# Prompt attention in one inference step: a third score buffer, another order of ScalarE's copies, one head's weighting on GpSimd

## The chip, the cores and the metric

The kernel runs on one core of a Trainium2 chip. The metric is the device time in microseconds, the median of several runs. The engines are TensorE (PE), VectorE (DVE), ScalarE (ACT), GpSimd (POOL) and SyncE (SP), which here only issues DMAs.

## What is computed

One layer of a decoder for 1024 prompt tokens and 8 x 4 sample tokens: a gated MLP mixer beside a sparse attention with three branches, an output projection, a cross attention, a gated MLP with a convolution. The change lies in the prompt's sparse attention. It has 8 query heads of width 64 and 2 key heads. Cut to what matters:

```python
l_cmp = einsum(q, kc) * scale + bias(d_cmp)        # 63 compressed keys
p_cmp = masked_softmax(l_cmp, d_cmp >= 0)
l_sel = einsum(q, k_sel) * scale + bias(d_sel)     # selected blocks, causal
p_sel = masked_softmax(l_sel, m_sel)
p_win = masked_softmax(einsum(q, k_band) * scale + bias(dist), 0 <= dist < 512)
out   = g0 * p_cmp @ vc + g1 * p_sel @ v_sel + g2 * p_win @ v_band
```

With 1024 tokens every causal block of 64 is among the selected ones, so the second branch is full causal attention.

## The kernel before

`program` runs phases one after the other, each a block of per-engine programs whose order is written out by hand and tied by semaphores: input, gating, compression, `sample_attention` (L633), `prompt_attention` (L835), then the output mix and the rest. A barrier ends each block.

**The steps.** `prompt_attention` works through 32 steps (`STEPS`, L852). Step m has a head pair j (0 to 3: query heads j and j + 4, called head g = 0 and g = 1) and a query block i of 128 tokens. For even j, i goes 0 to 7, for odd j 7 to 0. One head of a step has a score row of up to 1727 columns in SBUF: (i+1) x 128 "far" scores (second branch), min(i+1, 5) x 128 window scores and 63 compressed ones, the last two together called "near". In blocks of up to 128 columns that is 3, 5, 7, 9, 11, 12, 13 and 14 blocks for i = 0 to 7. `groups` (L861) cuts them into groups of four: one to three groups for i up to 5, four for i = 6 and 7.

**What each engine does in pass m** (loops over m at L946, L992 and L1039):

- PE: transposes of head 1 of step m-2 (`turn`, L928), near scores of m (L913, L917), the product with the values of m-2 (`multiply`, L941), far scores of m+1 (L901), transposes of head 0 of step m-1.
- DVE: `far` adds the bias to the far scores of m for both heads and takes the minimum (`add`, L961), from PSUM to the score buffer `sc`; `weigh` for head 0 of m-1: a reciprocal (L985) and three TENSOR_SCALAR (L988) that multiply the exponents by 1/sum and the gate; `close` adds the bias to the near scores of both heads (two adds each, L961); `weigh` for head 1 of m-1.
- ACT: copies of the transposed head 1 of m-2 from PSUM to SBUF (`copy`, L1027, L1030), exponents of head 0 of m (three ACTIVATE, L1018), the finished output of m-2 (L1037), copies of head 0 of m-1, exponents of head 1 of m. As written, the copy of head 1 of a step thus stands behind the exponents of head 1 of the next step.

**Buffers.** Scores land in PSUM banks 0 to 3, far and near in the same ones: near scores wait for `far_taken` (both far adds done), far scores of the next step for `near_taken` (all close adds done). Transposes go to banks 4 to 6, one group each: the group with number t waits until the group t-3 is copied (L926). Outputs are in bank 7. `sc` has two buffers for each head (L844), so `far` of step n waits until the transposes of the same head of step n-2 are done (L967).

**Strips.** The bias comes as strips, 960 KB and 320 KB for each head (`near`, `inside`), one set for each head pair, from `bias_rows` in DRAM (L879, L880). SP issues the sets of j = 0 and 1 at the start of the block, then the reload of x (L885, three DMAs, needed by the output mix), then the sets of j = 2 and 3 when their places are free. In the block before, SP issues page loads (`gather`) only; PE there computes products for two halves of the samples (L726) and counts them in `pv`.

The lines that say most:

```python
pe.wait_ge(copied, t - 2)                                                       # L926, t >= 3
dve.wait_ge(turned, turns[n - 2, g, len(groups(n - 2)) - 1] + 1)                # L967, n >= 2
```

Of the kernel before, what the change touches and what calls it, by code (L numbers as in the profile page):

```python
# [632 lines left out]
def sample_attention(nc, K, I):  # L633
# [27 lines left out]
    with nc.Block() as block:  # L661
        @block.sync
        def _(sp):
            gather(sp, K, 1, "sel")

# [168 lines left out]

def prompt_attention(nc, K, I):  # L835
# [4 lines left out]
    near = [[ar[:, 2560 * g:2560 * g + STRS] for g in range(2)],  # L840
            [ar[:, 5120 + STRS * g:5120 + STRS * (g + 1)] for g in range(2)]]
    inside = [[ar[:, 2560 * g + STRS:2560 * (g + 1)] for g in range(2)],
              [K.top[:, O_CP + 192 + STRW * g:O_CP + 192 + STRW * (g + 1)] for g in range(2)]]
    sc = [[ar[:, 8960 + 1728 * (2 * b + g):8960 + 1728 * (2 * b + g + 1)] for g in range(2)] for b in range(2)]  # L844
    pt = [x.rearrange("p (b n) -> p b n", b=14) for x in (K.top[:, O_TMP:O_TMP + 1792], ar[:, 15872:17664])]
    sta = [[ar[:, 17664 + 16 * (2 * b + g):17664 + 16 * (2 * b + g + 1)] for g in range(2)] for b in range(2)]
    strip_came = [S(f"pa_strip{b}") for b in range(2)]
    far_done, far_taken, near_done, near_taken = S("pa_far"), S("pa_far_taken"), S("pa_near"), S("pa_near_taken")
    minima, exps, probs = S("pa_minima"), S("pa_exp"), S("pa_probs")
# [23 lines left out]
    with nc.Block() as block:  # L873
        @block.sync
        def _(sp):
            def strip(j):
                for g in range(2):
                    base = (j + 4 * g) * (VECS + VECW)
                    sp.dma_start(near[j % 2][g], bass.AP(K.vec_dram.tensor, base, [[1, P], [1, STRS]])).then_inc(strip_came[j % 2], 16)  # L879
                    sp.dma_start(inside[j % 2][g], bass.AP(K.vec_dram.tensor, base + VECS, [[1, P], [1, STRW]])).then_inc(strip_came[j % 2], 16)  # L880

            strip(0)
            strip(1)
            for a, b in PIECES:
                sp.dma_start(K.XT[:, :, a:b], I["xt"][:, :, a:b]).then_inc(K.x_came, 16)  # L885
            for j in range(2, 4):
                sp.wait_ge(near_taken, 8 * (j - 1))
                strip(j)

        @block.tensor  # L890
        def _(pe):
# [29 lines left out]
            def turn(n, g):  # L921
                pe.wait_ge(probs, 2 * n + g + 1)
                for k, (_, bl) in enumerate(groups(n)):
                    t = turns[n, g, k]
                    if t >= 3:
                        pe.wait_ge(copied, t - 2)  # L926
                    for x, (col, w, _, _) in enumerate(bl):
                        last = nc.tensor.transpose(K.bank[4 + t % 3][:w, x * P:(x + 1) * P], sc[n % 2][g][:, col:col + w], K.ident[:, :])  # L928
# [30 lines left out]
        def _(dve):  # L959
# [4 lines left out]
            def far(n, g):  # L964
                j, i = STEPS[n]
                if n >= 2:
                    dve.wait_ge(turned, turns[n - 2, g, len(groups(n - 2)) - 1] + 1)  # L967
                w = (i + 1) * P
                return add(sc[n % 2][g][:, 0:w], K.ps[:, 1024 * g:1024 * g + w], near[j % 2][g][:, 895 + w:895:-1], sta[n % 2][g][:, 1:2])

            def close(n, g):
                j, i = STEPS[n]
                s, m, strip = sc[n % 2][g], sta[n % 2][g], near[j % 2][g]
                w = min(i + 1, 5) * P
                top = 992 + P * i
                add(s[:, 1024:1024 + w], K.ps[:, 1024 * g:1024 * g + w], inside[j % 2][g][:, w - 1::-1], m[:, 2:3])
# [3 lines left out]
            def weigh(n, g):  # L980
                j, i = STEPS[n]
                s, m = sc[n % 2][g], sta[n % 2][g]
# [7 lines left out]
                last.then_inc(probs, 1)  # L990

            for n in range(N):  # L992
                j, i = STEPS[n]
                if n % 8 == 0:
                    dve.wait_ge(strip_came[j % 2], 64 * (j // 2 + 1))
# [14 lines left out]

        @block.scalar
        def _(act):
            def exp(n, g):
                _, i = STEPS[n]
                s, m = sc[n % 2][g], sta[n % 2][g]
# [23 lines left out]
            for m in range(N + 2):  # L1039
                if m >= 2:  # L1040
                    copy(m - 2, 1)
# [4 lines left out]
                if 1 <= m <= N:  # L1046
                    copy(m - 1, 0)
                if m < N:
# [846 lines left out]
def program(nc, I, O):  # L1895
    ctx = ExitStack()
    with ctx:
# [56 lines left out]
        K.sample_o = K.big[:, BIG - 256:BIG].rearrange("p (h n) -> p h n", h=2)  # L1954
        K.pools = {"cmp": I["pool_cmp"], "sel": I["pool_sel"]}
# [207 lines left out]
```

## Time and profile before

| | us |
|---|---|
| median of 3 runs (lowest, highest) | 2157.05 (2155.07, 2157.63) |
| the profiled execution's own time | 2156.39 |
| its span, first to last instruction | 2154.6 |
| PE busy in the span | 1960.8 (91%) |
| DVE / ACT / POOL busy | 851.6 / 507.4 / 221.4 |
| mean granted TensorE clock (1 is 2.4 GHz) | 0.958 |

Times in rows count from the span's start. The prompt attention runs from about 473 to 791 us, some 15% of the span. An interval between the near scores of two steps is the unit in which it moves. Matmul ends are modelled, so the start of the next instruction tells more than a duration.

### The profile page before, as it was taken

What the parts mean: (1) busy time and instruction counts of PE and PEld (TensorE: products, weight loads), DVE (VectorE), ACT (ScalarE), POOL (GpSimd) and SP (SyncE); (2) the same over time, 40 slices, a digit from 0 to 9 for tenths busy, and PEclk for the clock granted to TensorE, in tenths of its full rate; (3) what the DMA queues carried; (4) which work ended last, traced back from release to release, by engine and by line L of the source; (5) the groups of instructions that cost most, each with busy time, mean ns of one, the idle gap of its engine ahead of it and who ended that gap; (6) DMA issues with size and microseconds to landing.
All of it is one profiled execution on the core that took longest, in us unless ns stands there. A gap on an engine that the chain in (4) does not pass through costs nothing. (4 is left out here: it accounts for less than half of the span.)

```text
span 2154.6 us, 26289 instructions
## 1 busy us (share of the span) xinstructions
PE 1960.8 (91%) x10926; PEld 1548.8 (72%) x10926; DVE 851.6 (40%) x1832; ACT 507.4 (24%) x1103; POOL 221.4 (10%) x98
## 2 busy tenths in 40 slices
PE   7989998748788869989988899999999999999997
PEld 4555547535565546565658446899999999999997
DVE  3001214236567553530004113455545555545547
ACT  2112221006577561100112102121101111111112
POOL 0000000000000000000000000043223332233230
PEclk9999999867899889999999999999999999999999
DMA  5511006723110020031121600111011110111012
GB/s 208 148 63 71 0 0 168 216 96 112 50 50 1 1 99 39 1 126 60 30 97 40 265 28 0 37 66 54 25 40 59 59 50 11 59 59 59 20 44 81
DMA packets 97003, 145.12 MB, mean 67 GB/s; under 512 B 40622, under 2 KB 73454, under 8 KB 94990
## 3 DMA queue, kind: packets, MB, share of 16 engines
q1 hardware_dynamic: 92798, 140.30, 19.2%
q10 hardware_dynamic: 4088, 3.17, 0.5%
q8 instruction: 86, 1.41, 0.3%
q14 instruction: 31, 0.25, 0.0%
HBM read 132.37 MB, written 14.19 MB: 68 GB/s over the span
## 5 line engine op out<-in xcount | busy, mean ns | idle before, releaser
L1619 PE MATMUL ps<-ff_in_high,ff_weights_low 128*128 128x352 f32 x1056 | 342.6, 324 | 0.0
L1619 PE MATMUL ps<-ff_in_high,ff_weights_high 128*128 128x352 f32 x1056 | 340.2, 322 | 0.0
L1619 PE MATMUL ps<-ff_in_low,ff_weights_high 128*128 128x352 f32 x1056 | 338.0, 320 | 0.0
L1619 PEld LDWEIGHTS ps<-ff_in_high,ff_weights_high 128*128 128x128 f32 x1056 | 198.8, 188 | 0.3
L1619 PEld LDWEIGHTS ps<-ff_in_low,ff_weights_high 128*128 128x128 f32 x1056 | 198.3, 188 | 0.2
L1619 PEld LDWEIGHTS ps<-ff_in_high,ff_weights_low 128*128 128x128 f32 x1056 | 198.1, 188 | 0.0
L1823 DVE TENSOR_TENSOR x<-ps,x 128x352 f32<-128x352 f32 x216 | 113.4, 525 | 134.5 <-PE ps L1637 134.5
L373 PE MATMUL ps<-big 128*128 128x512 f32 (+3 forms) x432 | 160.8, 534 | 6.2 <-DVE top L406 6.2
L1637 PE MATMUL ps<-ff_act_high,ff_down_high 128*128 128x352 f32 (+1 forms) x496 | 158.3, 319 | 0.2
L1637 PE MATMUL ps<-ff_act_high,ff_down_low 128*128 128x352 f32 (+1 forms) x496 | 156.6, 316 | 0.0
L1637 PE MATMUL ps<-ff_act_low,ff_down_high 128*128 128x352 f32 (+1 forms) x496 | 156.5, 316 | 0.0
L1588 POOL TENSOR_TENSOR ff_weights_low<-ff_weights,ff_weights_high 128x1024 fp32r<-128x1024 f32 x44 | 106.0, 2410 | 471.9 <-ACT ff_weights_high L1719 471.9
L373 PEld LDWEIGHTS ps<-big 128*128 128x128 f32 (+1 forms) x432 | 78.8, 183 | 87.1 <-issue 79.9
L1018 ACT ACTIVATE big<-big 128x63 f32<-128x63 f32 (+8 forms) x192 | 114.4, 601 | 77.7 <-DVE big L961 77.4
L1227 PE MATMUL ps<-big 128*128 128x352 f32 x384 | 122.0, 478 | 7.5 <-DVE big L1161 5.5
L961 DVE CUSTOM_DVE_ANT_0 big<-ps,big 128x63 f32<-128x63 f32 (+8 forms) x160 | 81.7, 536 | 109.6 <-PE ps L928 92.5
L1688 PE MATMUL ps<-big 128*128 128x352 f32 x384 | 115.6, 463 | 1.3 <-PEq L1429 1.3
L265 PE MATMUL ps<-big,top 128*128 128x352 f32 x384 | 115.1, 460 | 0.9 <-DMA top<-in_w_fm 0.9
L1273 PE MATMUL ps<-big,top 128*128 128x352 f32 x384 | 113.8, 459 | 0.0
L1227 PEld LDWEIGHTS ps<-big 128*128 128x128 f32 x384 | 75.4, 198 | 50.6 <-issue 8.1
L265 PEld LDWEIGHTS ps<-big,top 128*128 128x128 f32 x384 | 72.5, 190 | 44.8 <-ACT top L238 3.4
L1688 PEld LDWEIGHTS ps<-big 128*128 128x128 f32 x384 | 73.7, 192 | 42.6 <-issue 2.7
(273 smaller groups left out, 2901.7 us busy)
## 6 DMA issues: line engine op xcount, KB each, us to landing
ff_weights<-in_w_up SPq DMA_DIRECT2D x22, 512.0 KB, 4.1
ff_weights<-in_w_gate SPq DMA_DIRECT2D x22, 512.0 KB, 4.3
ff_down<-in_w_down SPq DMA_DIRECT2D x22, 512.0 KB, 3.5
x<-in_xt SPq DMA_DIRECT2D x6, 1408.0 KB, 14.3
big<-bias_rows SPq DMA_DIRECT2D x8, 960.0 KB, 7.7
top<-in_mem_kt SPq DMA_DIRECT2D x7, 1024.0 KB, 11.0
big<-in_w_tm SPq DMA_DIRECT2D x8, 652.0 KB, 16.5
top<-in_mem_v SPq DMA_DIRECT2D x5, 1024.0 KB, 17.3
```

What stands on the lines that cost most here:

```text
L265: last = nc.tensor.matmul(K.bank[3 * (c % 2) + p][:, 0:b - a], ring[:, c % 2, k, :], K.HT[:, k, a:b], start=k == 0, stop=k == KD - 1)
L373: last = nc.tensor.matmul(K.bank[3 * (t % 2) + s][:r, 0:b - a], K.HT[:, k, t * P:t * P + r], w[:, k, a:b], start=k == 0, stop=k == KD - 1)
L961: return nc.vector.tensor_tensor_reduce(out=out, in0=scores, in1=bias, scale=1.0, scalar=3e38, op0=ALU.add, op1=ALU.min, accum_out=least)
L1018: nc.scalar.activation(s[:, x:y], s[:, x:y], ACT.Exp, bias=m[:, b:b + 1], scale=-1.0, accum_out=m[:, 8 + b:9 + b]).then_inc(exps, 1)
L1227: last = nc.tensor.matmul(K.bank[n % 4][:, 0:b - a], w[:, c, k, :], K.HT[:, k, a:b], start=k == 0, stop=k == KD - 1)
L1273: last = nc.tensor.matmul(K.bank[QB[c % 2][p]][:, 0:b - a], xq_ring[:, c % 2, k, :], K.HT[:, k, a:b], start=k == 0, stop=k == KD - 1)
L1588: nc.gpsimd.tensor_tensor(w_low[:, s], landing[:, s], w_high[:, s], ALU.subtract).then_inc(low_done[s], 1)
L1619: last = nc.tensor.matmul(K.bank[3 * s + x][:, 0:b - a], wt[:, s, ws], h[:, k, a:b], start=k + n == 0, stop=k == KD - 1 and n == 2)
L1637: last = nc.tensor.matmul(bank[:, 0:b - a], wt[:, at], x[:, c % SLOTS, a:b], start=first and e + m == 0, stop=end and c == chunks[-1] and ...
L1688: last = nc.tensor.matmul(K.bank[(6, 7, 1, 4)[n % 4]][:, 0:b - a], w[:, c, k, :], K.HT[:, k, a:b], start=k == 0, stop=k == KD - 1)
L1823: nc.vector.tensor_tensor(K.XT[:, o, a:b], K.bank[6 + n % 2][:, 0:b - a], K.XT[:, o, a:b], ALU.add).then_inc(down_taken, 1)
```

## The change

It touches four things. The score buffers `sc` and the statistics become three per head (`SC = 3`), and `far` waits for step n-3. ACT copies head 1 of m-1 right behind head 0 of m-1, ahead of the exponents of head 1 of m. The three TENSOR_SCALAR of head 1 move to a new GpSimd program; DVE keeps the reciprocal, and `probs` becomes one semaphore for each head. And the places are laid out anew: strips of even j go to x's place (`K.first_strips`), so the first set is issued in the sample attention's SP program once the first product there is done, and the reload of x comes last, after 24 steps. Also, `multiply` of n waits for the output copy of n-1 where it waited for n-4.

```diff
@@ sample_attention
         def _(sp):
             gather(sp, K, 1, "sel")
+            sp.wait_ge(pv, 1)
+            bias_strips(sp, K, 0, *K.first_strips)
...
+def bias_strips(sp, K, j, near, inside, came):
+
+    for g in range(2):
+        base = (j + 4 * g) * (VECS + VECW)
+        sp.dma_start(near[g], bass.AP(K.vec_dram.tensor, base, [[1, P], [1, STRS]])).then_inc(came, 16)
+        sp.dma_start(inside[g], bass.AP(K.vec_dram.tensor, base + VECS, [[1, P], [1, STRW]])).then_inc(came, 16)
...
+    first = K.first_strips
+    strips = (first, second, first, second)
+    SC = 3
...
-            strip(0)
-            strip(1)
+            bias_strips(sp, K, 1, *strips[1])
+            for j in range(2, 4):
+                sp.wait_ge(near_taken, 8 * (j - 1))
+                bias_strips(sp, K, j, *strips[j])
+            sp.wait_ge(near_taken, 24)
             for a, b in PIECES:
                 sp.dma_start(K.XT[:, :, a:b], I["xt"][:, :, a:b]).then_inc(K.x_came, 16)
-            for j in range(2, 4):
-                sp.wait_ge(near_taken, 8 * (j - 1))
-                strip(j)
...
             def turn(n, g):
-                pe.wait_ge(probs, 2 * n + g + 1)
+                pe.wait_ge(probs[g], n + 1)
...
             def multiply(n):
-                if n >= 4:
-                    pe.wait_ge(o_taken, n - 3)
+                if n:
+                    pe.wait_ge(o_taken, n)
...
             def far(n, g):
                 j, i = STEPS[n]
-                if n >= 2:
-                    dve.wait_ge(turned, turns[n - 2, g, len(groups(n - 2)) - 1] + 1)
+                if n >= SC:
+                    dve.wait_ge(turned, turns[n - SC, g, len(groups(n - SC)) - 1] + 1)
...
             def weigh(n, g):
...
                 nc.vector.reciprocal(m[:, 12:15], m[:, 8:11]).then_inc(factors, 1)
+                if g:
+                    return
                 dve.wait_ge(factors, 2 * n + g + 1)
...
-                last.then_inc(probs, 1)
+                last.then_inc(probs[0], 1)
...
+        @block.gpsimd
+        def _(pool):
+            for n, (j, i) in enumerate(STEPS):
+                s, m = sc[n % SC][1], sta[n % SC][1]
+                pool.wait_ge(factors, 2 * n + 2)
+                for b, x, y in ((1, 0, (i + 1) * P), (2, 1024, 1024 + min(i + 1, 5) * P), (0, 1664, 1664 + NCMP)):
+                    last = nc.gpsimd.tensor_scalar(s[:, x:y], s[:, x:y], m[:, 12 + b:13 + b], K.GS[:, j + 4, i, b:b + 1],
+                                                   ALU.mult, ALU.mult)
+                last.then_inc(probs[1], 1)
...
             for m in range(N + 2):
-                if m >= 2:
-                    copy(m - 2, 1)
                 if m < N:
                     exp(m, 0)
                 if m >= 2:
                     out(m - 2)
                 if 1 <= m <= N:
                     copy(m - 1, 0)
+                    copy(m - 1, 1)
                 if m < N:
                     exp(m, 1)
```

How the order moves, at the two places on which most rests. First ACT, pass m = 24: L1018 is an exponent, L1037 the output of step 22, L1027 and L1030 copies of step 23, to `top` for head 0 and to `big` for head 1. Before:

```order
L1018 ACTIVATE big<-big 128x1024 [waits pa_minima]
L1018 ACTIVATE big<-big 128x640
L1018 ACTIVATE big<-big 128x63
L1037 ACTIVATE top<-ps 128x128 [waits pa_pv]
L1027 COPY top<-ps 128x512 [waits pa_turned] x3
L1027 COPY top<-ps 128x128 [waits pa_turned]
L1030 COPY top<-ps 63x128
L1018 ACTIVATE big<-big 128x1024 [waits pa_minima]
L1018 ACTIVATE big<-big 128x640
L1018 ACTIVATE big<-big 128x63
L1027 COPY big<-ps 128x512 [waits pa_turned] x3
```

The same place in the changed kernel (its lines are 16 further on):

```order
L1034 ACTIVATE big<-big 128x1024 [waits pa_minima]
L1034 ACTIVATE big<-big 128x640
L1034 ACTIVATE big<-big 128x63
L1053 ACTIVATE top<-ps 128x128 [waits pa_pv]
L1043 COPY top<-ps 128x512 [waits pa_turned] x3
L1043 COPY top<-ps 128x128 [waits pa_turned]
L1046 COPY top<-ps 63x128
L1043 COPY big<-ps 128x512 [waits pa_turned] x3
L1043 COPY big<-ps 128x128 [waits pa_turned]
L1046 COPY big<-ps 63x128
L1034 ACTIVATE big<-big 128x1024 [waits pa_minima]
```

The copies of head 1 moved ahead of the exponents of the next step's head 1.

Second DVE, from the last close add of step 22 to the far adds of step 23 (ISA is the custom add; the row without an input reads its minimum). Before:

```order
L961 ISA big<-ps,big 128x63
L961 ISA big 128x1
L985 RECIPROCAL big<-big 128x3 [waits pa_minima,pa_exp]
L988 TENSOR_SCALAR big<-big,gates_by_head 128x768 [waits pa_factors]
L988 TENSOR_SCALAR big<-big,gates_by_head 128x640
L988 TENSOR_SCALAR big<-big,gates_by_head 128x63
L961 ISA big<-ps,big 128x1024 [waits pa_turned,pa_far]
```

The changed kernel:

```order
L965 ISA big<-ps,x 128x63
L965 ISA big 128x1
L989 RECIPROCAL big<-big 128x3 [waits pa_minima,pa_exp]
L965 ISA big<-ps,x 128x1024 [waits pa_turned,pa_far]
```

Head 1's three multiplications left DVE's queue, and the wait on `pa_turned` now means step 20 where it meant step 21.

## Rows read from the trace of the kernel before

**Rows 1.** Windows view of three stretches: length, busy us (count) of five engines, PEclk, DMA.

```profile
484.00:791.00 307.00, 253.32 (x2284) 184.53 (x2284) 186.34 (x636) 201.82 (x632) 0.00 (x0) 0.90 0.11 39
637.00:688.00 51.00, 42.15 (x384) 28.81 (x384) 39.04 (x139) 38.33 (x130) 0.00 (x0) 1.00 0.09 33
716.00:722.00 6.00, 5.50 (x38) 4.36 (x40) 4.54 (x16) 1.68 (x4) 0.00 (x0) 0.50 0.00 0
```

**Rows 2.** Waits view, 484 to 791 us: us in total, times, longest.

```profile
DVE big L961 <- PE ps L928: 92.5, 52, 4.4
...
PE ps L913 <- DVE big L961: 37.5, 32, 9.6
...
PE ps L928 <- ACT big L1027: 14.3, 8, 1.9
```

**Rows 3.** Timeline of PE, 678 to 702 us: start us, us, engine, line, operation, idle before.

```profile
678.06 1.35 PE L913 MATMUL ps<-top 64*128 64x512 f32 x8 [1.19 <-DVE big L961]
...
684.13 3.00 PE L928 MATMUL ps<-ident,big 128*128 128x128 f32 x24
688.46 1.35 PE L913 MATMUL ps<-top 64*128 64x512 f32 x8 [1.33 <-DVE big L961]
...
689.91 0.32 PE L941 MATMUL ps<-top 128*64 128x128 f32 x1
...
692.83 1.99 PE L901 MATMUL ps<-top 64*128 64x512 f32 x8
694.74 1.65 PE L928 MATMUL ps<-ident,big 128*128 128x128 f32 x13
...
699.95 0.32 PE L928 MATMUL ps<-ident,big 128*63 128x128 f32 x1 [1.79 <-ACT big L1027]
701.59 1.02 PE L913 MATMUL ps<-top 64*128 64x512 f32 x2 [1.33 <-DVE big L961]
```

**Rows 4.** Timeline of DVE and ACT, 689 to 702 us.

```profile
691.70 0.26 DVE L961 CUSTOM_DVE_ANT_0 big<-ps,big 128x63 f32<-128x63 f32 x1
...
697.03 1.16 ACT L1018 ACTIVATE big<-big 128x1024 f32<-128x1024 f32 x1
...
699.32 1.54 ACT L1027 COPY big<-ps 128x512 f32<-128x512 f32 x3
...
700.30 1.23 DVE L961 CUSTOM_DVE_ANT_0 big<-ps,big 128x1024 f32<-128x1024 f32 x1 [2.49 <-PE ps L928]
```

**Rows 5.** Timeline of PE: near scores that start intervals 7, 11, 27 and 31.

```profile
540.54 0.70 PE L913 MATMUL ps<-top 64*128 64x512 f32 x2 [1.33 <-DVE big L961]
...
598.42 1.13 PE L913 MATMUL ps<-top 64*128 64x512 f32 x4 [0.92 <-DVE big L961]
...
746.28 1.22 PE L913 MATMUL ps<-top 64*128 64x512 f32 x2 [0.92 <-DVE big L961]
...
779.19 0.49 PE L913 MATMUL ps<-top 64*128 64x128 f32 x4 [0.39 <-DVE big L961]
```

**Rows 6.** Timeline around the stage's start: PE, SP and DVE.

```profile
448.51 2.00 PE L726 MATMUL ps<-top,big 32*32 32x128 f32 x56
...
473.63 0.36 SPq L879 DMA_DIRECT2D big<-bias_rows  x1
...
483.25 0.29 DVE L961 CUSTOM_DVE_ANT_0 big<-ps,big 128x128 f32<-128x128 f32 x1 [9.89 <-DMA big<-bias_rows]
...
483.82 0.79 PE L913 MATMUL ps<-top 64*128 64x128 f32 x3 [9.65 <-DVE big L961]
```

**Rows 7.** Timeline of PE, 643 to 645 us: far scores with 384 columns.

```profile
643.89 0.92 PE L901 MATMUL ps<-top 64*128 64x384 f32 x4
```

**Rows 8.** Groups by form: instructions of DVE and GpSimd; busy us, mean ns of one.

```profile
L988 DVE TENSOR_SCALAR big<-big,gates_by_head 128x1024 f32<-128x1024 f32 x8 | 6.5, 813 | 0.3
...
L1588 POOL TENSOR_TENSOR ff_weights_low<-ff_weights,ff_weights_high 128x1024 fp32r<-128x1024 f32 x44 | 106.0, 2410 | 471.9 <-ACT ff_weights_high L1719 471.9
...
L1328 POOL MEMSET top<- 128x2048 f32 x1 | 1.8, 1805 | 710.8 <-POOLq L1083 710.8
```

More of the change, by code:

```diff
@@ L839, in prompt_attention @@
     ar = K.big[:, O_HT:BIG]
[L840 to L847, printed above, removed]
+    first = K.first_strips
+    second = ([ar[:, STRS * g:STRS * (g + 1)] for g in range(2)],
+              [ar[:, 2 * STRS + STRW * g:2 * STRS + STRW * (g + 1)] for g in range(2)], S("pa_strip1"))
+    strips = (first, second, first, second)
+    SC = 3
+    sc = [[ar[:, 5120 + 1728 * (2 * b + g):5120 + 1728 * (2 * b + g + 1)] for g in range(2)] for b in range(SC)]
+    pt = [x.rearrange("p (b n) -> p b n", b=14) for x in (K.top[:, O_TMP:O_TMP + 1792], ar[:, 15488:17280])]
+    sta = [[ar[:, 17280 + 16 * (2 * b + g):17280 + 16 * (2 * b + g + 1)] for g in range(2)] for b in range(SC)]
     far_done, far_taken, near_done, near_taken = S("pa_far"), S("pa_far_taken"), S("pa_near"), S("pa_near_taken")
-    minima, exps, probs = S("pa_minima"), S("pa_exp"), S("pa_probs")
+    minima, exps, probs = S("pa_minima"), S("pa_exp"), [S(f"pa_probs{g}") for g in range(2)]
     factors = S("pa_factors")
@@ L927, in turn @@
                     for x, (col, w, _, _) in enumerate(bl):
-                        last = nc.tensor.transpose(K.bank[4 + t % 3][:w, x * P:(x + 1) * P], sc[n % 2][g][:, col:col + w], K.ident[:, :])
+                        last = nc.tensor.transpose(K.bank[4 + t % 3][:w, x * P:(x + 1) * P], sc[n % SC][g][:, col:col + w], K.ident[:, :])
                     last.then_inc(turned, 1)
             def multiply(n):
-                if n >= 4:
-                    pe.wait_ge(o_taken, n - 3)
+                if n:
+                    pe.wait_ge(o_taken, n)
                 gs = groups(n)
@@ L965, in far @@
                 j, i = STEPS[n]
-                if n >= 2:
-                    dve.wait_ge(turned, turns[n - 2, g, len(groups(n - 2)) - 1] + 1)
+                if n >= SC:
+                    dve.wait_ge(turned, turns[n - SC, g, len(groups(n - SC)) - 1] + 1)
                 w = (i + 1) * P
-                return add(sc[n % 2][g][:, 0:w], K.ps[:, 1024 * g:1024 * g + w], near[j % 2][g][:, 895 + w:895:-1], sta[n % 2][g][:, 1:2])
+                return add(sc[n % SC][g][:, 0:w], K.ps[:, 1024 * g:1024 * g + w], strips[j][0][g][:, 895 + w:895:-1], sta[n % SC][g][:, 1:2])
             def close(n, g):
                 j, i = STEPS[n]
-                s, m, strip = sc[n % 2][g], sta[n % 2][g], near[j % 2][g]
+                s, m, strip = sc[n % SC][g], sta[n % SC][g], strips[j][0][g]
                 w = min(i + 1, 5) * P
                 top = 992 + P * i
-                add(s[:, 1024:1024 + w], K.ps[:, 1024 * g:1024 * g + w], inside[j % 2][g][:, w - 1::-1], m[:, 2:3])
+                add(s[:, 1024:1024 + w], K.ps[:, 1024 * g:1024 * g + w], strips[j][1][g][:, w - 1::-1], m[:, 2:3])
                 return add(s[:, 1664:1664 + NCMP], K.ps[:, 1024 * g + 640:1024 * g + 640 + NCMP],
@@ L994, in _ @@
                 if n % 8 == 0:
-                    dve.wait_ge(strip_came[j % 2], 64 * (j // 2 + 1))
+                    dve.wait_ge(strips[j][2], 64 * (j // 2 + 1))
                 dve.wait_ge(far_done, n + 1)
@@ L1014, in exp @@
                 _, i = STEPS[n]
-                s, m = sc[n % 2][g], sta[n % 2][g]
+                s, m = sc[n % SC][g], sta[n % SC][g]
                 act.wait_ge(minima, 2 * n + g + 1)
```

9 lines of the change are left out of this document (3 added, 6 removed).

## The prediction

> **What bounds the kernel now.** The windows view comes first: what does the prompt attention have to give [rows 1]? From 484 to 791 us PE is busy 253 of 307 us, ACT 202, DVE 186, POOL 0, at a mean granted clock of 0.90. No engine is full, so waits decide. The waits view of the same stretch says which [rows 2]: DVE's add (L961) waits 92.5 us for transposes (L928), the near scores on PE (L913) wait 37.5 us for DVE's add, and transposes wait 14.3 us, in eight places, for ACT's copies (L1027).
>
> One wide interval shows how they hang together. Steps are counted m = 0 to 31, with i the query block (8 steps per head pair, i rising, then falling), and an interval runs from near scores of m to those of m+1. From 688.46 to 701.59 (m = 23, i = 7) PE does near scores of 23, the product of 21, far scores of 24 and both transposes of 22 [rows 3]. All but the last transpose is done by 698.16 (699.95 - 1.79). The last one belongs to a fourth group of head 1. It needs a bank that ACT frees with the first copy of that head (L1027 at 699.32), and this copy stands behind the three exponents that began at 697.03 [rows 4]. PE idles 1.79 us. Only then may DVE overwrite the score buffer: its add starts at 700.30, takes 1.23, and the near scores wait for it, 1.33 us more [rows 3, 4]. Only i = 6 and 7 have four groups (13 and 14 blocks), so this happens after steps 6 to 9 and 22 to 25: intervals 7 to 10 and 23 to 26. They last 57.88 us (540.54 to 598.42) and 57.82 us (688.46 to 746.28) [rows 3, 5], **115.7 us together, a mean of 14.5**. In several of them the granted clock falls as well: it is 0.50 in 716 to 722, right after such a stop [rows 1].
>
> The stage's start is a DMA wait: SP issues the first strip at 473.63 and DVE's first add starts at 483.25, after 9.89 us idle [rows 6].
>
> **The sum.** All steps together: from the near scores of step 0 (483.82) to those of step 31 (779.19) the change has 31 intervals of 295.4 us to work on [rows 5, 6].
>
> *1. What PE itself needs at full clock.* From rows 3: near scores 688.46 to 689.91 = 1.45; product of 12 blocks 689.91 to 692.83 = 2.92, 0.243 a block; far scores with 1024 columns 692.83 to 694.74 = 1.91; 24 transposes 3.00, or 2.93 without the last one's tail, 0.122 each. Far scores with 384 columns take 0.92 against 1.99 for 1024 [rows 3, 7], so 0.21 per 128 columns; near scores shrink at the same rate below 640 columns, to 1.23, 1.03, 0.82, 0.60 for i = 3 to 0. Blocks per step are 3, 5, 7, 9, 11, 12, 13, 14 for i = 0 to 7, 74 a head pair. Over 31 intervals: near 37.3, products 281 x 0.243 = 68.3, far 37.1, transposes 576 x 0.122 = 70.3: 213.0 us.
>
> *2. What stays in the way.* Far and near scores share PSUM banks 0 to 3, so far scores still wait until both heads' close adds are done, and near scores until both far adds are. Wide: the close adds end 3.50 us after the near scores start (691.96) [rows 4], 2.05 after they end; the product (2.92) covers them. Narrow: it doesn't. Working this out for each i (near + 0.15 + close adds + 0.12 against near + product) costs 8.9 us over all steps. Where the DVE chain near, close, far, both far adds is longer than PE's work (i rising, 0 to 3) or the GpSimd chain of point 4 is, it adds another 4.1. Each interval also has a hand-off that no row names: interval 22 (678.06 to 688.46) is 10.40, PE's work in it 1.45 + 11 x 0.243 + 1.91 + 24 x 0.122 = 8.96, the last add 1.23, so 0.2 to 0.3; 0.25 x 31 = 7.8. And the clock is still low in the first three intervals (they make part of the 0.10 that the stage's mean lacks), which I leave in: +6. Sum: 213.0 + 8.9 + 4.1 + 7.8 + 6 = **239.8 us against 295.4, 55.6 less**.
>
> In the eight wide intervals that is 76.5 + 2.0 = 78.5 instead of 115.7, 37.2 less; m = 23 by itself: 1.45 + 2.92 + 1.91 + 26 x 0.122 = 9.45 instead of 13.13. The other 18 us come from the rest, 0.3 to 3 us each, mostly because DVE's far adds now run beside the transposes.
>
> *3. Why the wait is gone: order on ACT and a third buffer.* ACT copies head 1 before the exponents of the next step's head 1, so the fourth group finds a bank. Behind these copies now stand exponents (2.3 us at i = 7, 697.03 to 699.32) [rows 4], needed by the reciprocal behind the next close adds, 3.6 us after the near scores start, against copies that end 0.5 after it and 2.3: 2.8. They fit with 0.8 to spare. ACT's own work in such an interval is 2 x 2.3 + 2 x 1.87 + 0.25 = 8.6 of 9.6, close under PE. A far add waits for the transposes of three steps ago, done long before. o_taken is now awaited one step back; that output copy stands ahead of ACT's copies in the pass before, so it costs nothing.
>
> *4. Head 1's weights on GpSimd.* DVE loses 96 TENSOR_SCALAR (813 ns for 1024 elements [rows 8]), all hidden. In its place stands a chain: near scores, both close adds, reciprocal, three GpSimd instructions, head 1's transposes. At m = 23 GpSimd may start 4.0 us after the near scores and PE wants head 1's probabilities at 1.45 + 2.92 + 1.91 + 1.59 = 7.9: 3.9 us of room for 896 + 640 + 63 elements. No row shows a GpSimd TENSOR_SCALAR. Bounds [rows 8]: MEMSET of 2048 takes 1805 ns, 0.88 an element, without an input; TENSOR_TENSOR of 1024 takes 2410 ns, 2.35 an element, with two inputs. One input lies between: I take 1.5 ns and 0.15 us fixed, 2.9 us here, which is hidden. At 0.88 the sum is 1 us less. At 2.35 (4.2 us) the chain is the longest almost everywhere and the sum **18.4 us more**.
> The Trainium skill (GPSIMD Engine Reference, Engine selection) calls GpSimd about twice as slow for two inputs but "1-input is roughly line-rate". No run here shows that; by it the sum would be the one with the lower bound.
>
> *5. Strips and x.* The first four strip DMAs move to SP behind the first half's product in the sample attention, which ends near 450.5 (448.51 + 2.00) [rows 6]; nothing else is queued there. A strip set lands within 9.6 us, so by about 461, and the first far adds need it at 474.2. **9.1 us less**. The second set is issued at 473.6 as ever, for step 8. The x reload (three DMAs) moves behind the strips of steps 16 to 31 and waits for 24 steps: eight are left before its first reader, over 60 us by the sums above, and a set of strips takes under 10. Nothing.
>
> *6. The end.* The last two passes (11.9 us) have the same chain with GpSimd's three small instructions in it: +0.5.
>
> Sum: -55.6 - 9.1 + 0.5 = -64.2. The profiled execution took 2156.39, which gives 2092.2; the median of the runs, 2157.05, is 0.7 above: **2093 us**.
>
> **Rivals.**
> *A. GpSimd at the two-input price.* +18.4: **2111**. For it: the instruction has two more operands, the per-partition factors. Against: only one long input.
> *B. The clock still falls.* Eight intervals keep near scores and product at 1.2 GHz, as in 716 to 722 [rows 1]: six us at half clock lose 3 us of work, some stretches are shorter, so 2.5 each, +20: **2113**. For: PE still has short stops. Against: the clock is at 0.50 behind stops of 1.8 and 1.3 us close together, which go, and at 1.00 through all of 637 to 688 [rows 1], where only stops such as the 1.19 at 678.06 stand [rows 3].
> *C. DVE and GpSimd shut each other out.* DVE's TENSOR_SCALAR of 1024 takes 813 ns, an add of 1024 takes 1.23 us [rows 4, 8]: DVE runs head 0's weights in a faster way. If one such set per step waited for the rest of GpSimd's, 0.5 us, +15: **2108**. By my times they miss each other: GpSimd ends near 6.9 us into interval 23, and DVE reaches its weights only behind the far adds, at 8.9.
> The Trainium skill (SBUF — State Buffer, Who interferes with whom) says DVE's tensor_scalar can take a port pair that GpSimd needs, as "an exclusive lock". No stretch of this stage has both engines, so the trace neither agrees nor disagrees.
> *D. Slower.* GpSimd's TENSOR_SCALAR is slow enough to be the stage's bound. One head has 35.8 thousand elements per partition over all steps, so each ns an element beyond 2.35 adds up to 35.8 us. The total gain is used up at about 2.35 + (64.2 - 18.4) / 35.8 = 3.6 ns, a 1024 piece of 3.7 us. At twice the two-input price, 4.7 ns, it is 2111 + 84 = **2195**. Against: 2410 ns is the dearer kind of work.
>
> **Chances.** Forecast (with GpSimd cheap or middling) 0.58, A 0.18, B 0.11, C 0.08, D 0.04, no change 0.01. The low end, 2080, is the sum with full clock from the start (-6), the cheap GpSimd (-1) and hand-offs of 0.1 us (-4.7). The high end, 2119, takes in A, B and C and some of their overlap. About 0.2% (4 us) is what a measurement can tell from no change: faster 0.95, same 0.01, slower 0.04.
>
> **What would show it.** Intervals 7 to 10 and 23 to 26 between 9 and 10.5 us, with no PE wait for L1043 longer than 0.5 us and the clock at 1.00 through them; the first far add within 1 us of the first far scores; GpSimd's three instructions within 3.2 us at i = 7 and done before PE ends head 0's transposes. Right in total but wrong in kind: PE waiting for GpSimd (A, D), DVE's TENSOR_SCALAR of 1024 longer than 0.82 us (C), windows at 0.50 beyond the start (B). A time over 2125 makes the working wrong.

## The result, and the profile after

| | before | after |
|---|---|---|
| median us of 4 runs each (lowest, highest) | 2157.10 (2155.07, 2157.63) | **2081.82** (2080.13, 2083.28) |
| ratio to before, 95% interval | | 0.9652 [0.9636, 0.9669] |
| the profiled execution's time, its span | 2156.39, 2154.6 | 2083.28, 2081.5 |
| near scores of step 0, of step 31 | 483.82, 779.19 | 473.58, 704.76 |
| end of the stage's last output copy | 791.05 | 715.61 |

The change saves 75.3 us, 11 more than the 64.2 forecast. The 31 intervals take 231.18 us instead of 295.37, so 64.2 of it is there (by chance the figure of the whole forecast); the stage starts 10.2 us earlier, and its tail, from step 31's near scores to the end of the last output copy, takes 1.0 us less (10.85 for 11.86). The page of the changed kernel shows PE busy 93% of a shorter span, and work on GpSimd from the tenth of the 40 slices on:

```profile
PE 1939.8 (93%) x10926; PEld 1534.3 (74%) x10926; DVE 810.6 (39%) x1736; ACT 505.3 (24%) x1103; POOL 283.6 (14%) x194
...
POOL 0000000002222200000000000313331333133320
PEclk9999999969999999999999999999999999999999
```

The windows view of the changed kernel, which answers to [rows 1] (length, busy us of PE, PEld, DVE, ACT and POOL, PEclk, DMA):

```profile
477.00:480.00 3.00, 1.54 (x8) 1.19 (x8) 2.26 (x13) 0.51 (x3) 0.00 (x0) 0.50 0.95 360
480.00:483.00 3.00, 2.79 (x10) 1.64 (x10) 1.37 (x8) 1.31 (x8) 1.27 (x3) 0.50 0.32 124
483.00:486.00 3.00, 3.00 (x22) 1.86 (x20) 1.72 (x9) 2.10 (x10) 0.00 (x0) 0.60 0.00 0
...
486.00:716.00 230.00, 219.94 (x2238) 163.09 (x2236) 138.67 (x505) 193.61 (x604) 60.95 (x93) 1.00 0.13 43
```

PE is now busy 96% of the stretch (219.94 of 230) where it was 83%, and the granted clock is 1.00 (2.4 GHz) from 486 us to the stage's end. Only the first three intervals are partly at 0.50 (1.2 GHz). The waits view of 473 to 716 us, against [rows 2]:

```profile
DVE big L965 <- PE ps L905: 54.5, 32, 2.7
...
DVE big L965 <- PE ps L921: 28.9, 32, 1.8
...
PE ps L905 <- DVEq L1011: 5.2, 9, 1.3
...
PE ps L932 <- POOL big L1023: 2.5, 5, 0.9
PE ps L932 <- ACT top L1043: 1.9, 8, 0.3
PE ps L917 <- DVE big L965: 1.6, 2, 0.9
```

Three things have gone: DVE waiting for transposes (92.5 us), transposes waiting for head 1's copies (14.3, no row any more), and the near scores waiting for DVE's add (37.5, now 1.6). DVE still waits, but for the scores that it works on, as it should when PE is the bound. What is left for PE is 5.2 us for the close adds ahead of far scores (L1011 is DVE's count behind them), 2.5 us for GpSimd, and little else. Interval 23, of which [rows 3, 4] showed the old form, is now this on PE (timeline: start, us, engine, line, operation, idle before):

```profile
637.19 1.35 PE L917 MATMUL ps<-top 64*128 64x512 f32 x8
...
638.64 0.32 PE L945 MATMUL ps<-top 128*64 128x128 f32 x1
...
641.56 1.99 PE L905 MATMUL ps<-top 64*128 64x512 f32 x8
643.47 1.66 PE L932 MATMUL ps<-ident,big 128*128 128x128 f32 x13
645.38 1.63 PE L932 MATMUL ps<-ident,big 128*128 128x128 f32 x13 [0.25 <-ACT top L1043]
646.94 1.24 PE L917 MATMUL ps<-top 64*128 64x512 f32 x6
```

and this on DVE, ACT and POOL:

```profile
643.69 1.23 DVE L965 CUSTOM_DVE_ANT_0 big<-ps,big 128x1024 f32<-128x1024 f32 x1 [2.67 <-PE ps L905]
...
646.05 1.56 ACT L1043 COPY big<-ps 128x512 f32<-128x512 f32 x3 [0.18 <-PE ps L932]
647.49 0.27 ACT L1046 COPY big<-ps 63x128 f32<-63x128 f32 x1
647.65 1.16 ACT L1034 ACTIVATE big<-big 128x1024 f32<-128x1024 f32 x1
...
641.12 2.34 POOL L1023 TENSOR_SCALAR big<-big,gates_by_head 128x896 f32<-128x896 f32 x3 [6.76 <-DVE big L989]
```

The far add starts at 643.69, beside the transposes, where it used to come after all of them. ACT copies head 1 first and begins the exponents behind (647.65). PE stops once, 0.25 us for a bank, and the interval takes 9.75 us instead of 13.13. GpSimd is done at 643.46, 1.7 us before head 0's transposes end (645.13).

### The profile page after: what moved, and what is told of

The parts are those of the page before. It is cut to its first block and busy times, and to the rows that moved or that the text cites. A ratio compares the mean times of both kernels' runs of the same rounds, so it can differ in the third digit from the quotient of the medians.

```text
span 2081.5 us, 26292 instructions
## 1 busy us (share of the span) xinstructions
PE 1939.8 (93%) x10926; PEld 1534.3 (74%) x10926; DVE 810.6 (39%) x1736; ACT 505.3 (24%) x1103; POOL 283.6 (14%) x194
## 5 line engine op out<-in xcount | busy, mean ns | idle before, releaser
L265 PEld LDWEIGHTS ps<-big,top 128*128 128x128 f32 x384 | 72.5, 190 | 44.9 <-ACT top L238 5.3
L1288 PEld LDWEIGHTS ps<-big,top 128*128 128x128 f32 x384 | 73.0, 190 | 40.9 <-issue 0.5
```

Of the source, the lines that this page charges most:

```text
L265: last = nc.tensor.matmul(K.bank[3 * (c % 2) + p][:, 0:b - a], ring[:, c % 2, k, :], K.HT[:, k, a:b], start=k == 0, stop=k == KD - 1)
L1288: last = nc.tensor.matmul(K.bank[QB[c % 2][p]][:, 0:b - a], xq_ring[:, c % 2, k, :], K.HT[:, k, a:b], start=k == 0, stop=k == KD - 1)
```

## The experiments

Each was timed beside the kernel before on the same chip, in three groups: runs of before had medians of 2154.9 (first group), 2154.2 (second) and 2155.1 (third). Diffs are against the changed kernel unless they say otherwise. Step numbers, intervals and line numbers are those of the changed kernel; where an edit shifts lines, the text says what a line is.

### Group 1: one part undone at a time

**Head 1's weights back on DVE.** Three buffers, the new ACT order and the early strips stay.

```diff
@@ weigh
-                if g:
-                    return
-                last.then_inc(probs[0], 1)
+                last.then_inc(probs[g], 1)
@@ the GpSimd program: removed
```

> The changed kernel with head 1's three multiplications back on DVE, behind its reciprocal. My theory (the third buffer, ACT's order and the early strips carry the gain; GpSimd carries none of it): 2083 to 2088 us, because in the wide intervals DVE has the weights done before the next far scores end, and only in narrow ones (i up to 3) the far adds start some 0.3 us later. Rival (taking work off DVE is part of the gain): 2095 or more. Other rival (GpSimd is a burden and DVE's weights come sooner): under 2080, and the 0.9 us stops of PE before the last transposes of steps 30 and 31 go.

Measured: **2077.33** (2076.84 to 2078.07), ratio 0.9642 [0.9629, 0.9655]. The theory's 2083 to 2088 is a miss, and the second rival is what happened. The median is *lower* than the changed kernel's, though the ratio intervals overlap ([0.9636, 0.9669] there). All intervals are as before the edit but those of the narrowest steps, 15 to 17: 4.42, 3.57, 4.23 instead of 4.67, 3.96, 4.28. The timelines say why. In the changed kernel in interval 15 (PE, then POOL):

```profile
590.83 0.77 PE L932 MATMUL ps<-ident,big 128*128 128x128 f32 x5
591.96 0.77 PE L932 MATMUL ps<-ident,big 128*128 128x128 f32 x5 [0.37 <-POOL big L1023]
...
590.42 1.49 POOL L1023 TENSOR_SCALAR big<-big,gates_by_head 128x256 f32<-128x256 f32 x3 [3.40 <-DVE big L989]
```

and with the weights on DVE:

```profile
591.53 1.65 PE L932 MATMUL ps<-ident,big 128*128 128x128 f32 x10
...
591.06 0.96 DVE L992 TENSOR_SCALAR big<-big,gates_by_head 128x256 f32<-128x256 f32 x3
```

The same three pieces take 0.96 us on DVE and 1.49 on GpSimd, and PE's transposes run through. Intervals 15 to 17 give 0.7 us and the tail, where the changed kernel stops PE for 0.88 and 0.82 us (0.20 and 0.31 here), another 1.2. These 1.9 us stand in the traces; the medians, taken on different chips, are 4.5 apart. DVE had room for its 96 instructions; relieving it was worth nothing.

**Two score buffers.**

```diff
-    SC = 3
+    SC = 2
```

> The changed kernel with two score buffers for each head instead of three. My theory: the near scores again wait for head 1's transposes plus one far add (0.2 to 1.2 us, 0.7 in the mean, and a hand-off of 0.25) in each of 31 intervals: about +25, 2107 us (2100 to 2114), intervals 23 to 26 near 11 us. Rival (ACT's order alone removes the wait, the buffer is an extra): 2082 to 2088.

Measured: **2112.07** (2111.02 to 2112.97), 0.9802 [0.9787, 0.9817], 30 above the changed kernel and inside what was expected. The wide intervals are 11.15, 11.14, 11.0 and 10.55, and the clock stays at 1.00 there. Its waits view has one PE wait that the changed kernel lacks, once in every step, and DVE waits for transposes again:

```profile
DVE big L965 <- PE ps L932: 106.3, 52, 4.4
...
PE ps L917 <- DVE big L965: 28.2, 32, 1.3
```

28.2 us of stops for 31 us more in the intervals (262.3 against 231.2). So the third buffer removes one wait per step, of about the last far add that stood between the last transpose and the near scores (1.3 us where that add takes 1.23).

**The old order of ACT's copies**, with three buffers.

```diff
             for m in range(N + 2):
+                if m >= 2:
+                    copy(m - 2, 1)
                 if m < N:
                     exp(m, 0)
...
                     copy(m - 1, 0)
-                    copy(m - 1, 1)
```

> The changed kernel with ACT's copies of head 1 again behind the exponents of the next step's head 1. My theory: PE stops about 1.8 us in the eight intervals that have a fourth group, +15, 2097 us (2092 to 2106, the high end if the clock falls again), other intervals as they are. Rival (with three buffers the order no longer matters): 2082 to 2085.

Measured: **2113.52** (2109.78 to 2119.44), 0.9819 [0.9802, 0.9836], well above all that was expected. The bank wait is there as expected, 14.3 us in eight places, but there is another one beside it, on the product (L945):

```profile
PE ps L945 <- ACT big L1043: 15.0, 20, 1.5
PE ps L932 <- ACT big L1043: 14.3, 8, 1.9
```

Interval 23 of this kernel shows both on PE's timeline:

```profile
656.59 1.35 PE L917 MATMUL ps<-top 64*128 64x512 f32 x8
...
658.73 0.29 PE L945 MATMUL ps<-top 128*64 128x128 f32 x1 [0.62 <-ACT big L1043]
...
668.76 0.32 PE L932 MATMUL ps<-ident,big 128*63 128x128 f32 x1 [1.79 <-ACT big L1043]
669.02 0.70 PE L917 MATMUL ps<-top 64*128 64x512 f32 x2
```

The product of a step needs all its transposes copied. With the old order head 1's copies stand behind exponents, and PE, which no longer stops for DVE, now reaches the product before they are done. With two buffers nearly all of this wait was covered by the near scores' own. The waits view of the kernel before has only this of it, two of the four places in the tail:

```profile
PE ps L941 <- ACT big L1027: 3.4, 4, 1.5
```

A third buffer with the old order turns 3.4 us in 4 places into 15.0 in 20. The expectation left that out. It did name the clock, and in this profile, the shortest of the four executions, the clock falls too: over 546 to 572 us, where intervals 9 and 10 lie, it averages 0.87, and they take 13.53 and 12.95 us, against 11.92 and 11.32 for intervals 25 and 26, alike but at 1.00. That is 3.2 of the 31 us, and rival B of the prediction in small. The other executions, up to 9.7 us longer, have no profile.

**Strips at the block's start** as before, all else changed.

```diff
-            sp.wait_ge(pv, 1)
-            bias_strips(sp, K, 0, *K.first_strips)
@@ prompt_attention
         def _(sp):
+            bias_strips(sp, K, 0, *strips[0])
```

> The changed kernel with the first set of strips issued at the start of the prompt attention as before. Theory: the first far add starts 10 us later, everything behind it by as much: 2092 us (2090 to 2093). Rival (the rest catches up, or the clock at the start pays it back): under 2088.

Measured: **2090.68** (2089.35 to 2091.65), 0.9702 [0.9687, 0.9717], as expected, 9 us above the changed kernel. That is a net figure: in the profiles the near scores of step 0 come 10.1 us later and the 31 intervals take 233.0 us instead of 231.2, but the part behind the stage, where nothing was edited, happens to be 3.6 us shorter. DVE's first add waits for the DMA again:

```profile
483.13 0.29 DVE L964 CUSTOM_DVE_ANT_0 big<-ps,x 128x128 f32<-128x128 f32 x1 [9.75 <-DMA x<-bias_rows]
```

In the changed kernel it starts at 473.01, 0.65 us after the first far scores (472.36).

### Group 2: parts alone, and a way to mend the cost

**The changed kernel once more**, so that the group has it on its own chip. 

> The changed kernel as it is, on the chip of the next three. 2081 us, or 2079 if the 2.5 us by which its first profile was longer behind the prompt attention belonged to that chip; ratio to the kernel before 0.965.

Measured: 2081.18 (2081.04 to 2084.76), 0.9668 [0.9655, 0.9681].

**Weights on DVE, and PE waiting on the minima** themselves in place of the count that DVE sets after them.

```diff
-                    pe.wait_ge(near_taken, n)
+                    pe.wait_ge(minima, 2 * n)
...
                 close(n, 1).then_inc(minima, 1)
-                dve.wait_ge(minima, 2 * n + 2)
-                dve.sem_inc(near_taken, 1)
@@ weigh for both heads, no GpSimd program; SP waits on minima too
```

> The changed kernel with head 1's weights back on DVE, and with far scores and strips waiting for DVE's close adds themselves (minima) instead of the extra DVE wait and signal (near_taken). Theory: 1 to 3 us under the changed kernel on the same chip: 2.0 from the weights (the two 0.9 us stops at the end and 0.7 in intervals 15 to 17), up to 1 from the hand-off in the dozen narrow intervals that the DVE chain sets. Rival (the 2 us were another chip's): within 1 us of the changed kernel.

Measured: **2077.61** (2076.24 to 2082.47), 0.9652 [0.9638, 0.9666], 3.6 us under the changed kernel on this chip, where 1 to 3 were expected, with ratio intervals that overlap a little. The narrow intervals lose 0.05 to 0.07 each; 229.89 us for the 31, 1.2 less than the changed kernel there (231.05). Nothing else is gained by the shorter hand-off.

**The new ACT order alone, in the kernel before.**

```diff
@@ before
             for m in range(N + 2):
-                if m >= 2:
-                    copy(m - 2, 1)
...
                     copy(m - 1, 0)
+                    copy(m - 1, 1)
```

> The kernel before with nothing changed but ACT's order: copies of both heads ahead of the exponents of the next step's head 1. If the parts add up: the old order cost 31 us in the changed kernel, so 2124 us. My theory: the 1.8 us stops and the late product go, the last far add stays on the path: 2122 (2118 to 2130), intervals 23 to 26 near 11.1 as with two buffers in the changed kernel, since GpSimd plays no part.

Measured: **2118.78** (2117.95 to 2119.62), 0.9838 [0.9823, 0.9853]: 35.4 us under before for three moved lines, as expected. The 31 intervals take 262.5.

**The third buffer alone, in the kernel before**, with the places that it needs, strips at the block's start and both heads' weights on DVE. (It also keeps the semaphores per head and the earlier wait of `multiply`.)

```diff
@@ before
+    SC = 3
...
-                if n >= 2:
-                    dve.wait_ge(turned, turns[n - 2, g, len(groups(n - 2)) - 1] + 1)
+                if n >= SC:
+                    dve.wait_ge(turned, turns[n - SC, g, len(groups(n - SC)) - 1] + 1)
```

> The kernel before with the third score buffer alone (strips of even head pairs in x's place, but the first set issued at the stage's start, x reloaded late; old order on ACT, weights on DVE). If the parts add up: 30 us under the kernel before, 2125. Theory: the same stops as with the old order in the changed kernel, so 2113.5 + 9 for the strips - 2 for the weights = 2120 (2116 to 2126). A rival (buffer and order need each other) would have it above 2135.

Measured: **2124.07** (2123.29 to 2129.28), 0.9868 [0.9851, 0.9886]: 30.1 under before, as expected. Its waits view holds the same two rows as that of the old copy order above, the product's wait and the banks':

```profile
PE ps L944 <- ACT big L1030: 15.0, 20, 1.5
PE ps L931 <- ACT big L1030: 14.3, 8, 1.9
```

The parts add up: 35.4 + 30.1 = 65.5, and both together with late strips gave 64.2 (the kernel with late strips against before). The match is no closer than a few us: that kernel also pays for GpSimd, and the third buffer alone loses some 8 us to the clock, since its intervals 9, 10 and 24 to 26 take 1.6 us each more than their like at a clock of 1.00 in the run with the old order (13.53 against 11.92 for i = 6), at a mean of 0.87 to 0.88.

### Group 3: how much room GpSimd's chain has

**Both heads' weights on GpSimd.**

```diff
@@ weigh: DVE keeps the reciprocals only
             for n, (j, i) in enumerate(STEPS):
+                for g in range(2):
...
+                    last.then_inc(probs[g], 1)
```

> The changed kernel with head 0's weights on GpSimd as well (DVE does adds and reciprocals only). My theory (neither engine bounds the stage, GpSimd's sets of 1.3 to 2.4 us fit one behind the other): 2081 to 2085 us, wide intervals unchanged at 9.75 to 9.9, and DVE's 35 us of freed time bring nothing. Rival (DVE's queue holds the near scores or the close adds up): under 2078. Rival (GpSimd is at its limit with one head): over 2090.

Measured: 2081.98 (2080.23 to 2084.49), 0.9658 [0.9644, 0.9673], as expected and as the changed kernel, interval by interval. Head 0's weights have room on either engine, and DVE's free time buys nothing.

**GpSimd 1.13 us later in each step**: two MEMSETs of 600 elements of unused space ahead of the three multiplications.

```diff
                 pool.wait_ge(factors, 2 * n + 2)
+                for u in range(2):
+                    if n:
+                        pool.wait_ge(pad[u], n)
+                    nc.gpsimd.memset(ar[:, 17400 + 600 * u:18000 + 600 * u], 0.0).then_inc(pad[u], 1)
```

> The changed kernel with two fills of 600 elements ahead of GpSimd's set in every step, 1.2 us more (0.6 each by the fill of 2048 in 1.8). It measures the room that the prediction gave GpSimd: wide intervals (room of 1.8 us in the trace of the changed kernel: set done at 643.46, head 1's transposes begun near 645.2) stay; narrow ones (i up to 3) grow by up to 0.9, the two stops at the end by 1.2 each: 2088 to 2096. Rival (no room anywhere): +1.2 in each step, 2120. Other rival (room everywhere): 2084.

Measured: **2100.18** (2099.57 to 2100.45), 0.9742 [0.9727, 0.9757], 18 above the changed kernel and over the 2088 to 2096 that were expected. The wide intervals did not move (9.00, 9.76, 9.88, 9.88, 9.55), as their 1.7 us of room says. The narrowest ones, 14 to 18, grew by 1.1 to 2.1 us each, interval 16 from 3.96 to 5.14 and interval 18, at a lower clock, from 5.29 to 7.42, because they had next to no room, and the tail by 3.2; the others but the first grew by 0.2 to 1.7. PE's wait and, after its stops, the granted clock:

```profile
PE ps L933 <- POOL big L1028: 13.5, 15, 2.0
```

```profile
590.00:600.00 10.00, 7.37 (x87) 5.72 (x83) 4.97 (x30) 7.28 (x32) 5.62 (x10) 1.00 0.28 100
600.00:610.00 10.00, 8.76 (x70) 5.62 (x68) 5.30 (x32) 7.30 (x34) 4.38 (x10) 0.83 0.47 166
610.00:620.00 10.00, 9.22 (x47) 5.56 (x49) 4.90 (x20) 5.71 (x22) 3.33 (x7) 0.66 0.00 0
```

In 590 to 600 us PE is busy 7.37 of 10 at full clock, and in the next 20 us part of the time is at half clock. That second loss was not in the expectation. It is the mechanism of the prediction's rival B, here brought about by a wait in the narrow steps.

**The bank waits split by head**, first with GpSimd's weights, then with both on DVE: PE waits for one head's add before that head's scores, not for both.

```diff
                     for g in range(2):
+                        if n and not x:
+                            pe.wait_ge(minima, 2 * n - 1 + g)
...
+                        if not x:
+                            pe.wait_ge(far_taken, 2 * n + g + 1)
...
-                far(n, 0)
+                far(n, 0).then_inc(far_taken, 1)
```

> The changed kernel (head 1's weights on GpSimd) with PE's waits on the shared banks split by head: near scores of head 0 start once head 0's far add is done, far scores of head 0 once its close adds are. Theory that intervals with i up to 3 are set by the chain near scores, close adds, far scores, far adds: they shrink by 0.2 to 0.6 each, wide ones stay, 2074 to 2079. Rival (they are set by PE's own work and hand-offs): within 1 us of 2081.

> The same split with head 1's weights on DVE. If the split shortens the chain, DVE's own 1.6 us of weights per head may now be in the way in narrow intervals, and GpSimd gain a use: 2072 to 2078; better than the version with GpSimd by about 2 (the stops at the end) if DVE is not in the way, equal or worse if it is.

Measured: 2080.73 (2080.30 to 2081.45), 0.9653 [0.9640, 0.9667] with GpSimd, and 2078.26 (2077.46 to 2082.60), 0.9646 [0.9633, 0.9660] with DVE. Both are a miss for the idea, and the first run's rival (within 1 us of 2081) is what happened: PE's waits for the close adds fall from 5.2 to 1.3 us, but the 31 intervals take 229.5 us against 231.2. Only intervals 0 and 2, at the start, are 0.7 us shorter with GpSimd's weights, the others change by less than 0.3. In the narrow steps PE still waits for GpSimd before the transposes (0.35 us in interval 15, where the changed kernel has 0.37):

```profile
593.39 0.77 PE L933 MATMUL ps<-ident,big 128*128 128x128 f32 x5 [0.35 <-POOL big L1022]
```

The lowest medians are those of the changed kernel without its GpSimd part: 2077.3 to 2078.3 us in three forms that these runs don't tell apart. That GpSimd costs something is shown by its stops in the traces, 1.9 us; the medians alone leave it open, since the ratio intervals overlap in each group. The plain one, weights back on DVE, has the fewest parts.

## Why the prediction was right, and where its terms were off

**The wait and what it set (sum, points 1 to 3): right.** The eight wide intervals were to take 78.5 us and took 78.14 (9.75, 9.88, 9.89, 9.55, twice), all between 9 and 10.5, at a granted clock of 1.00 and with no wait for L1043 over 0.3 us. The reason holds too: undoing either half (order or buffer) brings back waits of its own, and each costs about 30 us.

**The waits of point 2, +8.9 and +4.1: mis-sized.** In the 28 intervals from the fourth on (489.43 to 704.76) the sum had 220.0 us: 205.3 of PE's own work by point 1, 7.0 for hand-offs, and so 7.7 for waits for the close adds and for the DVE and GpSimd chain. They took 215.3. PE's waits in that stretch are 2.3 us in six places for the close adds (L1011), 0.8 in three for GpSimd (L1023) and 1.9 in eight for a bank (L1043). So the waits of point 2 are 3.1 us by name where 7.7 were taken. That difference alone is about the 4.7 by which these intervals beat the sum.

**Hand-offs, +7.8: about right in total, but not where it was put.** With 1.9 us of bank stops, 5.0 us are left for the 28 intervals if PE's own work is as in point 1. The 0.25 us were measured in interval 22 of the kernel before, which ended with the far add. That interval is now 9.00 us, PE's own work in it 8.96: the hand-off went with the add. In the wide intervals at most 0.16 is left beside bank stops, as in interval 23, where PE's own sum of 9.45 became 9.75 with a stop of 0.25. But intervals 3, 4 and 15 to 20 have 0.3 to 0.6 each that no row names; whether they are hand-offs or a part of point 2's waits stays open. A hand-off between two engines should be struck from a sum together with the work that it hands over.

**The first three intervals, +6 for the clock: mis-sized.** They were to take 19.8 us with it and took 15.85. The granted clock averages 0.81 over 473 to 500 us and is 1.00 from 486 on; in the kernel before it averages 0.57 there. How these 4.0 us divide between the clock and the waits isn't shown. With late strips the first intervals are 4.25, 5.88 and 7.63, 1.9 us more, and the mean over 473 to 500 is 0.57 again; so early strips and the clock at the start go together. The 4.7 and the 4.0 us are the 8.6 by which the 31 intervals beat the sum (rounded). Nearly all of the terms erred to the same side, and so the result lies near the low end that the prediction gave, 2080.

**Strips, -9.1: right.** The start moved by 10.2, of which 1.3 lies ahead of the stage (the first far scores come at 472.36 against 473.68), where the near scores of step 0 vary between 472.8 and 476.3 from run to run of kernels that are alike there. Undoing the early strips costs 9 us net.

**The end, +0.5: wrong sign.** The tail took 10.85 us against 11.86. The two stops for GpSimd are there, 0.88 and 0.82 us, more than the +0.5 that stood for them. But the kernel before has three stops for head 1's copies in its tail:

```profile
780.56 0.29 PE L941 MATMUL ps<-top 128*64 128x128 f32 x1 [0.70 <-ACT big L1027]
...
785.54 0.29 PE L941 MATMUL ps<-top 128*64 128x128 f32 x1 [1.50 <-ACT big L1027]
...
788.99 0.45 PE L941 MATMUL ps<-top 128*64 128x128 f32 x1 [0.71 <-ACT big L1030]
```

The first is gone in the changed kernel and the second is 0.66 us; the third is still 0.71. The granted clock, 0.68 over 785 to 791 us before, is 1.00 over 704 to 716. The prediction counted neither. With DVE's weights the tail is 9.65.

**GpSimd's price, 2.9 us in interval 23: too dear; hidden as said in the wide steps, not in all.** PE waits for GpSimd in five places, 2.5 us in all. By form, GpSimd and DVE in the changed kernel (busy us, mean ns of one):

```profile
L1023 POOL TENSOR_SCALAR big<-big,gates_by_head 128x1024 f32<-128x1024 f32 x4 | 4.8, 1198 | 29.7 <-DVE big L989 29.7
...
L1023 POOL TENSOR_SCALAR big<-big,gates_by_head 128x128 f32<-128x128 f32 x8 | 3.5, 454 | 81.0 <-DVE big L989 81.0
```

```profile
L994 DVE TENSOR_SCALAR big<-big,gates_by_head 128x1024 f32<-128x1024 f32 x4 | 3.3, 814 | 0.1
...
L994 DVE TENSOR_SCALAR big<-big,gates_by_head 128x128 f32<-128x128 f32 x8 | 2.4, 346 | 0.1
```

(1198 - 454) / 896 = 0.83 ns an element and 0.35 us fixed for each instruction; 1.5 and 0.15 were taken. The set of interval 23 (896 + 640 + 63) takes 2.34 us where 2.9 were taken, one at i = 7 2.45, one at i = 1 1.49. The fixed part, three times 0.35, is the term that matters, since it doesn't shrink in narrow steps, where the room does. DVE needs 0.52 an element ((814 - 346) / 896) and 0.28 fixed. For the price of an element the low bound, which MEMSET gave, was the right row. The Trainium skill (GPSIMD Engine Reference, Engine selection) has "1-input is roughly line-rate", and the trace agrees in kind: 0.83 ns against DVE's 0.52, not the 2.35 of two inputs.

**The rivals.** A (+18.4, GpSimd at 2.35) is out by that price. B didn't occur in the changed kernel. It isn't far: the clock fell in wide intervals with the old copy order and in narrow ones with GpSimd held back by 1.13 us. D would have needed 3.6 ns an element. C, DVE and GpSimd shutting each other out, was rightly taken as a matter of whether they meet. They seldom do: DVE's 1024 pieces take 814 ns against 813 [rows 8], and four of its 32 sets overlap one of GpSimd's, none of them lengthened (0.96 us at i = 1 and 0.83 at i = 0, as the others; GpSimd's beside the last one takes 1.58 us for 1.49). But the effect is real. In the run with GpSimd held back the sets meet in narrow steps, and DVE's, of 256 + 256 + 63 elements, is 0.40 us longer than the 0.96 that it takes alone, GpSimd's beside it 0.14 longer than 1.70:

```profile
592.37 1.36 DVE L995 TENSOR_SCALAR big<-big,gates_by_head 128x256 f32<-128x256 f32 x3
...
591.85 1.84 POOL L1028 TENSOR_SCALAR big<-big,gates_by_head 128x384 f32<-128x384 f32 x3
```

**What the working missed.** That DVE's relief would be worth nothing was said (point 4, "all hidden"), but that the move costs 2 to 4 us was not: the +4.1 of point 2 has the chain through GpSimd together with DVE's, and no sum with the weights left on DVE stands beside it. And point 3 looked for the copies' readers only in the banks; the product is the other one, and it was worth as much (15.0 against 14.3 us). A row of before hinted at it, 3.4 us in four places. It didn't spoil the forecast because both parts were changed together.

What stays open: the part behind the stage took 1363.6 us before and 1365.9 in the changed kernel's profile, and 1361.4 in that of the kernel with minima, though no edit is there; the same changed kernel had 1362.0 in its second profile. Such differences of 2 to 4 us are as large as GpSimd's cost by the medians, of which the traces show 1.9 us.

## What to carry to other kernels

Where two waits stand in a row on the bounding engine, look for the reader that comes next once they are gone: each half of this change was worth 30 to 35 us alone, but it left or uncovered a wait that only the other half removes. In an engine's queue put the work that frees a bank or feeds the bounding engine ahead of the work that has a step to spare; here three moved lines gave almost half of the gain. Work moved to a slower engine is to be priced in the *narrowest* step, by its fixed cost, where the chain has least room, and only moved if the engine it leaves is in the way.

## What the runs showed of the hardware

GpSimd's TENSOR_SCALAR with two per-partition factors: 0.83 ns an element, 0.35 us fixed; it is 1.5 times as long as DVE's at 1024 elements and 1.3 times at 128.

DVE and GpSimd can shut each other out for far longer than in this stage. In the last block of the changed kernel, which the change doesn't touch, DVE runs a TENSOR_SCALAR of 32 elements in 0.29 us when GpSimd is idle and in 2.37 when a TENSOR_TENSOR has just begun there (DVE, then POOL):

```profile
1615.83 2.37 DVE L1813 TENSOR_SCALAR ff_conv<-ff_row,ff_small 128x32 f32<-128x32 f32 x1
...
1638.89 0.29 DVE L1813 TENSOR_SCALAR ff_conv<-ff_row,ff_small 128x32 f32<-128x32 f32 x1
...
1612.96 2.40 POOL L1603 TENSOR_TENSOR ff_weights_low<-ff_weights,ff_weights_high 128x1024 fp32r<-128x1024 f32 x1 [5.77 <-ACT ff_weights_high L1734]
1615.31 2.84 POOL L1608 TENSOR_TENSOR ff_down_low<-ff_down,ff_down_high 128x1024 fp32r<-128x1024 f32 x1
1636.02 2.40 POOL L1603 TENSOR_TENSOR ff_weights_low<-ff_weights,ff_weights_high 128x1024 fp32r<-128x1024 f32 x1 [5.11 <-ACT ff_weights_high L1734]
```

It ends at 1618.20, when GpSimd's instruction does (1618.15). The trace of before has the same rows, so the prediction could have had them for rival C: they show a short DVE instruction waiting for a whole one of GpSimd's. The Trainium skill (SBUF — State Buffer, Who interferes with whom) says that DVE's tensor_scalar can need the port pair that it shares with GpSimd, and that whoever comes second is then blocked for the whole of the other's instruction. Here the trace agrees.

PE's granted clock fell from 1.00 to 0.83 and 0.66, means over 10 us each, behind stops of 0.86, 1.14 and 1.49 us in intervals of 6.5 to 5.1 us (the run with GpSimd held back). The length of a stop alone doesn't settle it: the clock was 1.00 through 637 to 688 us of the kernel before, with seven stops of up to 1.2 us for DVE's add, and through 531 to 575 us with two buffers, with a stop of 1.3 us in each wide interval.
